# A two-block transformer kernel: high weights against high part and remainder side by side in the narrow feed-forwards, and grouped attention with two buffers of turned probabilities

## The chip, the cores and the metric

The kernel runs on one core of a Trainium2 chip. The metric is the device time of one execution in microseconds (us), lower is better. A core has TensorE (PE, matrix products, with PEld for its weight loads), VectorE (DVE), ScalarE (ACT), GpSimd (POOL) and SyncE (SP, which issues most transfers).

## The reference

All tensors are float32. There are 256 latent tokens x, 256 context tokens, and model width 1024. A first part has two layers with modulated norms and residuals, and a second part has one layer:

```
layer 0: latent attention + pooling over x and ctx, then conv feed-forward on x and on ctx
layer 1: grouped attention (8 heads of 128, 2 key heads, queries from x, keys from ctx and x), then
         xl = xl + gate * conv_ffn(modulate(xl))          # x alone: 256 tokens
conv_ffn(h): a = h @ w_up; g, u = a[:, :2816], a[:, 2816:]
         return (silu(conv3(g) + b) * u) @ w_down
second block, x alone:
         x = x + 0.5 * rmsnorm((silu(h @ wg) * (h @ wu)) @ w_down1)
         x = x + mixer(x)                                 # differential and dilated attention, gates
         x = x + 0.5 * rmsnorm((silu(h @ wg2) * (h @ wu2)) @ w_down2)
```

Each attention is softmax(q k^T * scale) v, head by head. The output is x, 256 x 1024.

## The kernel before

**Products in three parts.** Every large product is taken in fp32r with both operands split into a high part and a remainder. `three` (L342) issues three matmuls for one 128x128 tile of weights: high weights by high activations, high weights by the remainder of the activations, remainder of the weights by high activations. The three add up in one place of PSUM. The remainder by the remainder is left out.

**Weights in stripes.** The weights come from memory in stripes of 1 MB (128 x 2048), 189 in all, through a ring of three slots. SP loads `w_raw` (`load`), ACT makes `w_hi` (`split_hi`, L320), DVE makes `w_lo` (`split_lo`, L324), PE multiplies. SP waits until DVE has split the slot's last stripe, ACT waits until PE has started the stripe behind it, DVE waits for ACT, and PE waits for DVE (`begin_stripe`). Each engine runs one fixed program, written out by hand and joined to the others by semaphores, so the order on an engine is the order of the text. On ACT and DVE the split of the stripe two ahead (`ahead_hi`, `ahead_lo`) stands between the steps of the stage at hand.

**Activations.** `h_hi` and `h_lo` are 8 tiles of 128 x 512, 256 columns for the context and 256 for x. Where only x is left, the high part lies in columns 256 to 511 of `h_hi` and the remainder in the same columns of `h_lo`.

**Feed-forwards.** There are four: 0 is wide (512 columns, both token sets), 1, 2 and 3 are narrow (256 columns). 1 has the convolution; 2 and 3 are those of the second block, whose norm factor `rinv` is multiplied in behind the product. Each has 11 pairs of hidden tiles, and a pair n takes three stripes: g (gate, 2 tiles by 8 steps of k), u (up, the same) and d (down, 2 by 8 tiles). PE works on them in the order g(n+1), u(n+1), d(n); in this document d0, g1 and so on are the stripes. `up_tensor` does g and u, `down_tensor` d; the pairs 1 to 9 are a hardware loop. A narrow g goes to PSUM bank 0 and u to bank 1, two tiles of 256 columns side by side.

DVE's turn per pair (`ffn_vector`) is: `a_lo(n)` (L1595), split of d, work on g (conv L1606 behind ACT's `ffn_mid_scalar` L1547, or `ffn_scale_vector` L1619), split of the next g, work on u (`ffn_prod_vector` L1626, L1630 or L1636), split of the next u. ACT has the silu and `a_hi` (L1530), which waits until PE has finished the d before.

**Between feed-forwards 1 and 2.** Feed-forward 2 starts on activations that are not normed yet (`join_*`); the last norm of the first block is folded into a factor. Behind pair 0, DVE does two side jobs in one go: `join_x_vector` (L588, the norm applied to X), and `tables_vector` (L1882 to L1901: angles of the rotation, then lambda), which waits in its middle for ACT's sine and exponentials (`tables_scalar`, with two loads of function tables).

**Grouped attention.** `gqa_in_*` makes q, k, v from 6 stripes, PE's last one (v) in two halves; norms and rotations of the vectors run on ACT and DVE. Then for each of 8 heads: scores (L1057, two banks), row maximum (DVE L1145), exponential (ACT L1108), division by the row sum (DVE L1159), turns through the identity (PE L1076), copy of the turned probabilities to `pt_gqa` (ACT L1119, `turned_scalar`), product with v (PE L1098, `gqa_out_tensor`), split of the output (ACT L1131, DVE L1136). `pt_gqa` is one buffer. On PE head h is turns(h), scores(h+2), out(h); on ACT exp(h+1), turned(h), out_hi(h). Then `out_tensor` multiplies by four stripes of `w_out` (GO to GO+3), and `gqa_out_vector` adds to X.

## Time and profile before

| | |
|---|---|
| median of 3 runs | 1711.71 us (1711.35 to 1713.31) |
| the profiled execution: time | 1712.31 us |
| the profiled execution: span | 1709.8 us |
| PE busy | 1623.4 us, 95% of the span, 10470 matmuls |
| PE weight loads | 1408.8 us, 82% |
| DVE busy | 1040.1 us, 61% |
| ACT busy | 697.7 us, 41% |
| moved by DMA | 257.65 MB, mean 151 GB/s |

Matmuls overlap in the profile: one of 256 columns shows 283 ns from start to end while the next one starts long before. The pace is therefore read from start to start. The span of the profiled execution is 2.5 us below its time; the sums of the prediction are made against the 1712.31 us.

### The profile page before, as it was taken

How to read it: one execution, taken by the hardware profiler on the slowest of the kernel's cores; microseconds unless marked ns; L12 is line 12 of the kernel's file. 1: busy time of each engine (PE TensorE's matmuls, PEld its weight loads, DVE VectorE, ACT ScalarE, POOL GpSimd, SP SyncE). 2: the span in 40 equal slices, each digit the busy share in tenths (PEclk: the TensorE clock that was granted, in tenths of full speed). 3: DMA queues.
4: the chain of work that ended last, by engine and by line, in shares of the span. 5: the costliest groups of instructions: out<-in, count | busy, mean ns of one | idle time of the engine just before them, and what ended most of it. 6: DMA issues, size and time to landing. Idle time of an engine off the chain costs nothing.

```text
span 1709.8 us, 25411 instructions
## 1 busy us (share of the span) xinstructions
PE 1623.4 (95%) x10470; PEld 1408.8 (82%) x10470; DVE 1040.1 (61%) x1310; ACT 697.7 (41%) x879; POOL 52.2 (3%) x102
## 2 busy tenths in 40 slices
PE   6999999999999989999999989998998989889997
PEld 4655658888778868689999989997998878889997
DVE  3446436788788666546656575555664665555554
ACT  3426324233222335445444644334334654353432
POOL 1150000000000000000000000000000000000000
PEclk8999999999999999999999999998999999999999
DMA  9730452345655313034555555553545223435551
GB/s 393 272 114 1 169 207 99 131 152 167 215 197 209 107 54 124 25 99 140 180 179 189 167 172 185 183 177 98 168 151 170 75 76 122 148 123 173 192 176 49
DMA packets 168682, 257.65 MB, mean 151 GB/s; under 512 B 4160, under 2 KB 148032, under 8 KB 161824
## 3 DMA queue, kind: packets, MB, share of 16 engines
q1 hardware_dynamic: 161232, 205.21, 36.5%
q0 software_dynamic: 7232, 51.12, 8.0%
q8 instruction: 55, 0.90, 0.2%
q10 hardware_dynamic: 144, 0.26, 0.1%
q14 instruction: 19, 0.16, 0.0%
HBM read 255.53 MB, written 1.05 MB: 150 GB/s over the span
## 4 chain that ended last, share of the span: by engine, by line
PE 84%; DVE 5%; issue 5%; ACT 4%; DMA 2%; POOL 0%; SPq 0%; DVEq 0%; ACTq 0%
PE psum L342 72%; PE psum L451 2%; DMA U<-in_mod_pieces 1%; PE psum L1098 1%; ACT w_hi L320 1%; PE psum L615 1%; DVE w_lo L324 1%; DMA U<-in_w_mod 1%; PE psum L1931 1%; PE psum L2203 1%; PE psum L2182 1%; DVE scr L484 1%; PE psum L2015 0%; DVE U L484 0%; PE psum L1076 0%
## 5 line engine op out<-in xcount | busy, mean ns | idle before, releaser
L342 PE MATMUL psum<-h_hi,w_hi 128*128 128x256 f32 (+1 forms) x2176 | 690.7, 317 | 31.2 <-DVE h_lo L497 13.2
L342 PE MATMUL psum<-h_lo,w_hi 128*128 128x256 f32 (+1 forms) x2176 | 676.5, 311 | 0.0
L342 PE MATMUL psum<-h_hi,w_lo 128*128 128x256 f32 (+1 forms) x2176 | 676.4, 311 | 0.0
L324 DVE TENSOR_TENSOR w_lo<-w_raw,w_hi 128x2048 fp32r<-128x2048 f32 x189 | 433.0, 2291 | 234.6 <-ACT w_hi L320 233.1
L342 PEld LDWEIGHTS psum<-h_hi,w_hi 128*128 128x128 f32 x2176 | 420.3, 193 | 78.0 <-issue 47.1
L320 ACT ACTIVATE w_hi<-w_raw 128x2048 fp32r<-128x2048 f32 x189 | 360.6, 1909 | 290.1 <-PE psum L342 288.6
L342 PEld LDWEIGHTS psum<-h_lo,w_hi 128*128 128x128 f32 x2176 | 420.7, 193 | 23.7 <-issue 4.3
L342 PEld LDWEIGHTS psum<-h_hi,w_lo 128*128 128x128 f32 x2176 | 420.4, 193 | 20.9
L342 PE MATMUL psum<-a_hi,w_hi 128*128 128x256 f32 (+1 forms) x720 | 224.7, 312 | 6.7 <-DVE w_lo L324 4.3
L342 PE MATMUL psum<-a_lo,w_hi 128*128 128x256 f32 (+1 forms) x720 | 223.3, 310 | 0.0
L342 PE MATMUL psum<-a_hi,w_lo 128*128 128x256 f32 (+1 forms) x720 | 223.1, 310 | 0.0
L342 PEld LDWEIGHTS psum<-a_hi,w_hi 128*128 128x128 f32 x720 | 137.6, 191 | 17.2 <-DVE w_lo L324 4.5
L342 PEld LDWEIGHTS psum<-a_hi,w_lo 128*128 128x128 f32 x720 | 137.6, 191 | 7.1
L342 PEld LDWEIGHTS psum<-a_lo,w_hi 128*128 128x128 f32 x720 | 137.7, 191 | 6.5
L1530 ACT ACTIVATE a_hi<-U 128x512 fp32r<-128x512 f32 x55 | 33.6, 628 | 203.8 <-PE psum L342 186.8
L1644 DVE SCALAR_TENSOR_TENSOR X<-psum,mod,X 128x256 f32<-128x256 f32 x176 | 75.0, 479 | 26.7 <-PE psum L342 26.7
L1606 DVE SCALAR_TENSOR_TENSOR U<-psum,par,U 128x510 f32<-128x510 f32 (+1 forms) x88 | 52.1, 613 | 46.8 <-ACT U L1547 44.6
L1547 ACT ACTIVATE U<-psum,par 128x512 f32<-128x512 f32 (+1 forms) x44 | 28.3, 670 | 112.8 <-PE psum L342 112.8
L1595 DVE TENSOR_TENSOR a_lo<-U,a_hi 128x512 fp32r<-128x512 f32 x55 | 37.1, 689 | 57.6 <-ACT a_hi L1530 57.5
L658 DVE SCALAR_TENSOR_TENSOR U<-U,silu_all 128x2048 f32<-128x2048 f32 x28 | 65.2, 2347 | 0.8
L342 PE MATMUL psum<-w_hi,h_hi 128*128 128x256 f32 x144 | 41.9, 291 | 0.0
L451 PE MATMUL psum<-scr,const 128*128 128x256 f32 (+1 forms) x128 | 37.9, 450 | 4.2 <-ACT scr L426 4.2
(268 smaller groups left out, 1354.3 us busy)
## 6 DMA issues: line engine op xcount, KB each, us to landing
w_raw<-in_ffn_w_up SPq DMA_DIRECT2D x44, 1024.0 KB, 5.1
w_raw<-in_w_gu SPq DMA_DIRECT2D x44, 1024.0 KB, 5.1
U<-in_w_mod POOLq DMA_DIRECT2D x40, 1024.0 KB, 6.0
w_raw<-in_w_in SPq DMA_DIRECT2D x29, 1024.0 KB, 5.3
w_raw<-in_ffn_w_down SPq DMA_DIRECT2D x22, 1024.0 KB, 5.0
w_raw<-in_w_down SPq DMA_DIRECT2D x22, 1024.0 KB, 5.0
U<-in_mod_pieces POOLq DMA_DIRECT2D x8, 1024.0 KB, 17.8
w_raw<-in_gqa_w_in SPq DMA_DIRECT2D x6, 1024.0 KB, 5.0
```

The lines of the kernel that those rows point to most:

```text
L320: nc.scalar.activation(w_hi[:, i % RING, :], w_raw[:, i % RING, :], ACT.Copy).then_inc(hi_made, 1)
L324: nc.vector.tensor_tensor(w_lo[:, i % RING, :], w_raw[:, i % RING, :], w_hi[:, i % RING, :].bitcast(F32), ALU.subtract).then_inc(lo_made, 1)
L342: return [nc.tensor.matmul(dst, x, y, start=start and q == 0, stop=stop and q == 2, skip_group_check=True) for q, (x, y) in enumerate(pairs)]
L451: made = nc.tensor.matmul(psum[:, norm_bank(n), 0:tokens], ones, sq[:, b * T:b * T + tokens], start=c == 0 and b == 0, stop=c == chunks(n) ...
L484: made = nc.vector.scalar_tensor_tensor(out=dst, in0=x, scalar=g, in1=r, op0=ALU.mult, op1=ALU.mult)
L615: made = nc.tensor.matmul(psum[32 * j:32 * j + 32, 7, :], silu_all[:, 2 * k:2 * k + 32], w[:, TT * j:TT * (j + 1)], start=k == 0, stop=k = ...
L658: made = nc.vector.scalar_tensor_tensor(out=acc, in0=w, scalar=silu_c[:, k, s:s + 1], in1=acc, op0=ALU.mult, op1=ALU.add)
L1530: nc.scalar.activation(a_hi[:, 1 if last else t, :], f_act[:, t, :], ACT.Copy).then_inc(f_ahi, 1)
L1547: made = nc.scalar.activation(dst, src, ACT.Identity, bias=par[:, 1 + layer, bass.ds(66 + tile, 1)], scale=par[:, 1 + layer, bass.ds(NFF + ...
L1595: nc.vector.tensor_tensor(a_lo[:, at, :], f_act[:, t, :], a_hi[:, at, :].bitcast(F32), ALU.subtract).then_inc(f_alo, 1)
L1606: made = nc.vector.scalar_tensor_tensor(out=dst[:, :, dst_at:dst_at + T - 1], in0=src[:, :, src_at:src_at + T - 1], scalar=par[:, 1 + laye ...
L1644: made = nc.vector.scalar_tensor_tensor(out=x, in0=psum[:, 4 + m % 3, block_cols(s)], scalar=mod[:, 0, 40 + m, s:s + 1], in1=x, op0=ALU.mu ...
```

## The change

1. **Narrow g and u.** In the norms that feed the narrow feed-forwards (3, 4 and 8) the remainder is no longer written to `h_lo`: `h_hi[:, m, 0:256]` holds the high part and `h_hi[:, m, 256:512]` the remainder (`h_place`). A new `beside` issues two matmuls for a tile of weights: high weights by all 512 columns into a whole bank, remainder of the weights by the 256 high columns into the first half of that bank. So g has banks 0 and 1, u banks 2 and 3, and each bank holds two sums that are still to be added. `narrow_sum_vector` adds them on DVE (a tensor_reduce over two blocks, 1024 elements read from PSUM, 512 written) and its semaphores `f_gsum`, `f_usum` free the banks. What reads g or u behind it reads SBUF in place of PSUM. The down products and feed-forward 0 are as before.
2. **Side jobs of feed-forward 2.** The one block behind pair 0 is cut in four: `join_x_vector` behind pair 0, the angles behind pair 1, the sums for lambda behind pair 2, the rest behind pair 3; `tables_scalar` on ACT stands behind pair 2. The hardware loop on ACT and DVE starts at pair 4 there.
3. **Grouped attention.** `pt_gqa` becomes two buffers. The scores of heads 0 and 1 move on PE between the halves of the last stripe of `gqa_in`, behind a wait for all rotations (`gi_fix` 24), and their exponentials on ACT behind the two copies of v. In the loop PE does turns(h), scores(h+2), out(h-1), ACT turned(h), exp(h+2), out_hi(h-1), DVE max(h+2), norm(h+2), out_lo(h-1). The first stripe of `w_out` is taken apart (`gqa_merge_tensor`): tiles 0 to 4 before the turns of head 7, tile 5 behind out(6), 6 and 7 behind out(7); `out_tensor` starts at the second stripe.

```
+        def h_place(n, m, s):
+
+            if n in (3, 4, 8):
+                return h_hi[:, m, 0:T], h_hi[:, m, T:TT]
+            return h_hi[:, m, block_cols(s)], h_lo[:, m, block_cols(s)]
...
+        def beside(bank, weight, k, done=None, first=False):
+
+            wh, wl = weight
+            made = nc.tensor.matmul(psum[:, bank, :], wh, h_hi[:, k, :], start=k == 0, stop=False,
+                                    skip_group_check=True)
+            if first and k == 0:
+                made.then_inc(stripe_started, 1)
+            made = nc.tensor.matmul(psum[:, bank, 0:T], wl, h_hi[:, k, 0:T], start=False, stop=k == KD - 1,
+                                    skip_group_check=True)
+            if done is not None and k == KD - 1:
+                made.then_inc(done, 1)
...
             for t in range(4):
                 made = nc.tensor.matmul(psum[:, 4 + h % 2, 0:T], v_gqa[:, t, P * (h // 4):P * (h // 4 + 1)],
-                                        pt_g[:, t, :], start=t == 0, stop=t == 3)
+                                        pt_g[h % 2][:, t, :], start=t == 0, stop=t == 3)
...
-            need(act, at_o, 2 * (h // 2) if cfg is MLA else 8 * cfg["base"] + h)
+            need(act, at_o, 2 * (h // 2) if cfg is MLA else 8 * cfg["base"] + h - 1)
...
+        def narrow_tensor(pe, f, what, i, j, done, between):
+
+            slot = i % RING
+            need(pe, f_usum if what == "u" else f_gsum, sums_before(f) + j)
+            bank = 2 if what == "u" else 0
...
+            if what == "g" and isinstance(j, int) and j == 0:
+                for k in range(KD):
+                    h_ready(pe, FFNS[f]["norm"])(k)
+                    for t in range(2):
+                        beside(bank + t, weight(k, t), k, done if t else None, t == 0)
+                return
+            for t in range(2):
+                for k in range(KD):
+                    beside(bank + t, weight(k, t), k, done if t else None, t == 0)
+                if t == 0:
+                    between()
+
+        def narrow_sum_vector(dve, f, what, j):
+
+            bank, made = (0, f_gsum) if what == "g" else (2, f_usum)
+            dve.wait_ge(f_g if what == "g" else f_u, unit_base(f) + j + 1)
+            at = 0 if what == "g" and FFNS[f]["layer"] is None else 1
+            if what == "u":
+                dve.wait_ge(f_conv, unit_base(f) + j + 1)
+            elif at:
+                need(dve, f_prod, unit_base(f) + j)
+            nc.vector.tensor_reduce(f_act[:, at, :].rearrange("p (s t) -> p s t", s=2),
+                                    psum[:, bank:bank + 2, :].rearrange("p s (x t) -> p s t x", x=2), AX.X,
+                                    ALU.add).then_inc(made, 1)
+            dve.wait_ge(made, sums_before(f) + j + 1)
...
         def ffn_scale_vector(dve, f, j):
 
-            base = unit_base(f) + j
-            dve.wait_ge(f_g, base + 1)
-            need(dve, f_alo, base)
-            nc.vector.tensor_tensor(f_act[:, 0, :].rearrange("p (s t) -> p s t", s=2), bank2(0), double(rinv[:, 0:T]),
-                                    ALU.mult).then_inc(f_conv, 1)
+            need(dve, f_alo, unit_base(f) + j)
+            narrow_sum_vector(dve, f, "g", j)
+            g = f_act[:, 0, :].rearrange("p (s t) -> p s t", s=2)
+            nc.vector.tensor_tensor(g, g, double(rinv[:, 0:T]), ALU.mult).then_inc(f_conv, 1)
...
-            pair(0)
-            if f == 2:
-                join_x_vector(dve)
-                tables_vector(dve)
+            first = 4 if f == 2 else 1
+            parts = [lambda: join_x_vector(dve), lambda: angles_vector(dve), lambda: lambda_sums_vector(dve),
+                     lambda: lambda_vector(dve)]
+            for n in range(first):
+                pair(n)
+                if f == 2:
+                    parts[n]()
...
+                        if t == 0:
+                            pe.wait_ge(gi_fix, 24)
+                            scores_tensor(pe, GQA, 0, gqa_scores)
+                            scores_tensor(pe, GQA, 1, gqa_scores)
...
                         nc.scalar.activation(v_gqa[:, 2 * (u - 6):2 * (u - 6) + 2, :], bank2(u % 4),
                                              ACT.Copy).then_inc(gi_evac, 1)
+                        exp_scalar(act, GQA, u - 6)
...
         def gqa_tensor(pe):
-            pe.wait_ge(gi_fix, 24)
             pe.wait_ge(gi_evac, 8)
-
-            scores_tensor(pe, GQA, 0, gqa_scores)
-            scores_tensor(pe, GQA, 1, gqa_scores)
             for h in range(8):
+                if h == 7:
+                    begin_stripe(pe, GO)
+                    pe.wait_ge(at_e, at_base(GQA, n_rows) + n_rows(GQA) * 7)
+                    gqa_merge_tensor(pe, range(5))
                 turns_tensor(pe, GQA, h)
                 if h + 2 < 8:
                     scores_tensor(pe, GQA, h + 2, gqa_scores)
-                gqa_out_tensor(pe, h)
+                if h:
+                    gqa_out_tensor(pe, h - 1)
+            gqa_merge_tensor(pe, (5,))
+            gqa_out_tensor(pe, 7)
+            gqa_merge_tensor(pe, (6, 7))
```

**How the order moves.** In the rows of order a name like `psum<-h_hi,w_hi` is output, then operands, and the number behind it the columns.

PE, feed-forward 1, start of the loop over pairs 1 to 9 with the stripe g, before:

```order
L1516 UNCONDITIONAL_BRANCH
L1516 ISA
L99 REGISTER_ALU
L342 MATMUL psum<-h_hi,w_hi 128x256
L342 MATMUL psum<-h_lo,w_hi 128x256
L342 MATMUL psum<-h_hi,w_lo 128x256
L342 MATMUL psum<-h_hi,w_hi 128x256
L342 MATMUL psum<-h_lo,w_hi 128x256
```

The same place now:

```order
L1569 UNCONDITIONAL_BRANCH
L1569 ISA
L99 REGISTER_ALU
L369 MATMUL psum<-h_hi,w_hi 128x512
L373 MATMUL psum<-h_hi,w_lo 128x256
L369 MATMUL psum<-h_hi,w_hi 128x512
L373 MATMUL psum<-h_hi,w_lo 128x256
```

Three instructions of 256 columns for a tile of weights have become one of 512 and one of 256.

PE, grouped attention, the scores (L1057, now L1077), turns (L1076, now L1096) and products with v (L1098, now L1118), before:

```order
L1057 MATMUL psum<-U 128x512 x4
L1076 MATMUL psum<-const,scr 128x128 x8
L1057 MATMUL psum<-U 128x512 x2
L1098 MATMUL psum<-U 128x256 x4
L1076 MATMUL psum<-const,scr 128x128 x8
L1057 MATMUL psum<-U 128x512 x2
L1098 MATMUL psum<-U 128x256 x4
```

And now; the first row here stands behind the second half of the v stripe, and the scores of heads 0 and 1 no longer stand at its head but 48 matmuls earlier, between the halves:

```order
L1096 MATMUL psum<-const,scr 128x128 x8
L1077 MATMUL psum<-U 128x512 x2
L1096 MATMUL psum<-const,scr 128x128 x8
L1077 MATMUL psum<-U 128x512 x2
L1118 MATMUL psum<-U 128x256 x4
L1096 MATMUL psum<-const,scr 128x128 x8
L1077 MATMUL psum<-U 128x512 x2
L1118 MATMUL psum<-U 128x256 x4
```

The product with v has moved from behind its own head's turns to behind those of the next head.

DVE, feed-forward 2, from pair 0's work behind g1 to the side jobs (L324 is the split of a stripe, L1619 and L1626 the scaling of g and u, L1630 their product), before:

```order
L324 TENSOR_TENSOR w_lo<-w_raw,w_hi 128x2048
L1626 TENSOR_TENSOR U<-psum,rinv 128x512
L1630 TENSOR_TENSOR U<-U 128x512
L324 TENSOR_TENSOR w_lo<-w_raw,w_hi 128x2048
L588 SCALAR_TENSOR_TENSOR X<-X,par,rinv 128x256 x8
L1882 CAST scr<-U 128x256
L1883 TENSOR_SCALAR scr<-scr,const 128x256
```

The same place now (L331, L1674, L1681, L1684), with the sums L1491 and the split of d1 between `join_x_vector` (L608) and what follows:

```order
L331 TENSOR_TENSOR w_lo<-w_raw,w_hi 128x2048
L1491 TENSOR_REDUCE U<-psum 128x512
L1681 TENSOR_TENSOR U<-U,rinv 128x512
L1684 TENSOR_TENSOR U<-U 128x512
L331 TENSOR_TENSOR w_lo<-w_raw,w_hi 128x2048
L608 SCALAR_TENSOR_TENSOR X<-X,par,rinv 128x256 x8
L1650 TENSOR_TENSOR a_lo<-U,a_hi 128x512
L331 TENSOR_TENSOR w_lo<-w_raw,w_hi 128x2048
L1491 TENSOR_REDUCE U<-psum 128x512
```

Two reductions have come in, and `a_lo` and the split of a stripe now stand right behind `join_x_vector`, where the tables stood.

## Rows read from the trace of the kernel before

**Rows 1.** The page, part 4: the chain that ended last, by line
```profile
PE psum L342 72%; PE psum L451 2%; DMA U<-in_mod_pieces 1%; PE psum L1098 1%; ACT w_hi L320 1%; PE psum L615 1%; DVE w_lo L324 1%; DMA U<-in_w_mod 1%; PE psum L1931 1%; PE psum L2203 1%; PE psum L2182 1%; DVE scr L484 1%; PE psum L2015 0%; DVE U L484 0%; PE psum L1076 0%
```

**Rows 2.** View by windows, 800 to 900 us: busy us (x instructions) by engine, PEclk, DMA share, GB/s
```profile
800.00:900.00 100.00, 100.00 (x836) 100.00 (x835) 57.36 (x53) 45.02 (x42) 0.00 (x0) 1.00 0.56 186
```

**Rows 3.** Timeline of PE in a narrow feed-forward, 56 starts apart: start us, us, engine, line
```profile
859.75 0.28 PE L342 MATMUL psum<-h_hi,w_hi 128*128 128x256 f32 x1
...
866.47 0.28 PE L342 MATMUL psum<-h_hi,w_lo 128*128 128x256 f32 x1
```

**Rows 4.** Timeline of PE in the wide feed-forward, 14 starts apart
```profile
399.79 0.39 PE L342 MATMUL psum<-a_hi,w_hi 128*128 128x512 f32 x1
...
402.97 0.39 PE L342 MATMUL psum<-a_hi,w_lo 128*128 128x512 f32 x1
```

**Rows 5.** DVE groups by line and form: xcount | busy us, mean ns | idle before
```profile
L324 DVE TENSOR_TENSOR w_lo<-w_raw,w_hi 128x2048 fp32r<-128x2048 f32 x189 | 433.0, 2291 | 234.6 <-ACT w_hi L320 233.1
...
L1145 DVE TENSOR_REDUCE small<-psum 128x1 f32<-128x512 f32 x32 | 21.2, 687 | 7.8 <-PE psum L1057 5.5 <-PE psum L1050 2.2
...
L1619 DVE TENSOR_TENSOR U<-psum,rinv 128x512 f32<-128x512 f32 x22 | 15.2, 691 | 17.9 <-PE psum L342 16.9 <-ACT rinv L547 0.9
...
L2264 DVE TENSOR_REDUCE small<-scr 128x1 f32<-128x768 f32 x8 | 7.3, 948 | 0.1
```

**Rows 6.** Timeline, end of the first narrow feed-forward, DVE and ACT
```profile
957.82 0.69 DVE L1595 TENSOR_TENSOR a_lo<-U,a_hi 128x512 fp32r<-128x512 f32 x1
...
959.49 1.92 ACT L320 ACTIVATE w_hi<-w_raw 128x2048 fp32r<-128x2048 f32 x1 [3.39 <-PE psum L342]
```

**Rows 7.** Timeline, start of the second narrow feed-forward: DVE, PE, ACT
```profile
979.07 0.69 DVE L1619 TENSOR_TENSOR U<-psum,rinv 128x512 f32<-128x512 f32 x1 [0.93 <-ACT rinv L547]
...
987.88 2.29 DVE L324 TENSOR_TENSOR w_lo<-w_raw,w_hi 128x2048 fp32r<-128x2048 f32 x1 [1.11 <-ACT w_hi L320]
...
996.49 3.25 DVE L588 SCALAR_TENSOR_TENSOR X<-X,par,rinv 128x256 f32<-128x256 f32 x8
...
1007.53 0.15 DVE L1901 TENSOR_SCALAR small<-par 128x1 f32<-128x1 f32 x1
...
1010.89 2.29 DVE L324 TENSOR_TENSOR w_lo<-w_raw,w_hi 128x2048 fp32r<-128x2048 f32 x1 [1.10 <-ACT w_hi L320]
...
1013.23 0.58 PE L342 MATMUL psum<-a_hi,w_hi 128*128 128x256 f32 x1 [4.31 <-DVE w_lo L324]
...
1020.68 0.63 ACT L1530 ACTIVATE a_hi<-U 128x512 fp32r<-128x512 f32 x1 [4.44 <-PE psum L342]
```

**Rows 8.** View by windows, just behind PE's wait
```profile
1014.00:1016.00 2.00, 2.00 (x12) 0.50 0.61 174
```

**Rows 9.** Chain of waits through grouped attention: start us, us, what
```profile
705.50 1.72 PE psum L1057 x4
...
707.22 1.73 PE psum L1098 x8
...
708.95 0.89 PE psum L1076 x8
...
716.52 1.99 PE psum L1098 x8
...
721.30 1.99 PE psum L1098 x8
...
735.64 2.96 PE psum L1098 x8
...
742.87 23.02 PE psum L342 x192
```

**Rows 10.** Timeline: DVE's last rotation; PE at the eighth head
```profile
694.58 0.69 DVE L1823 TENSOR_TENSOR U<-U,std 128x512 f32<-128x512 f32 x1
...
735.64 1.68 PE L1098 MATMUL psum<-U 128*128 128x256 f32 x5 [1.92 <-ACT U L1119]
```

**Rows 11.** Timeline, start of the third narrow feed-forward, DVE
```profile
1516.87 0.68 DVE L1619 TENSOR_TENSOR U<-psum,rinv 128x512 f32<-128x512 f32 x1
```

146 lines of the change are left out of this document (89 added, 57 removed).

## The prediction

> **What bounds the kernel now.** First the chain that ended last: 72% of the span are split products of PE, and no other line has over 2% [rows 1]. Then the windows: in the narrow feed-forwards PE and PEld are busy for all of 100 us while DVE is busy for 57.36 and ACT for 45.02 [rows 2]. So there the pace is PE's own, and only fewer or shorter PE instructions, or the removal of PE's waits, can shorten the program. Third, the pace itself, from start to start: 56 steps of 256 columns take 866.47 - 859.75 = 6.72 us, 120.0 ns each [rows 3]; 14 steps of 512 columns take 402.97 - 399.79 = 3.18 us, 227.1 ns each [rows 4]. At 2.4 GHz the columns alone are 106.7 and 213.3 ns, so each instruction carries 13.3 or 13.8 ns on top, whatever its width. Last the two places where PE is not dense: the start of feed-forward 2, where it waits 4.31 us for the split of d1 [rows 7], and grouped attention, where a head takes 721.30 - 716.52 = 4.78 us [rows 9].
>
> **Part 1, two matmuls for three.** A tile of weights costs 3 x 120.0 = 360.0 ns before and 227.1 + 120.0 = 347.1 ns now, 12.9 ns less. There are 3 feed-forwards x 22 stripes x 16 tiles = 1056 of them: 13.6 us. In the three first stripes PE is paced by the norm that makes its activations, so their 48 tiles (0.6 us) gain nothing: **-13.0 us**. The bounds: nothing, if the time above the columns belongs to the columns or to the load of weights in a way that a longer matmul doesn't save; 26 ns a tile (-27 us) if a 256-column matmul behind a 512-column one lost its 13.3 ns too. Both rows show the surplus at equal size for both widths, so I take the middle, and a span of 10 to 14.5 us.
> The Trainium skill speaks against this size: "TensorE: Matmul & The Clock Gate", section "Back-to-back issue gap", has a warm matmul take its columns by 2.4 GHz plus about 2.5 ns, so that one matmul fewer would save 2.5 ns and the whole part 2.6 us. The trace disagrees in its premise: it has 13.3 ns where the page has 2.5 [rows 3].
>
> What it adds is the sums on DVE, 66 of them. A reduction of 512 elements from PSUM takes 687 ns and one of 768 takes 948 [rows 5], so 1.02 ns per element, and 1024 elements make **1.21 us**. Two of them raise DVE's busy time per pair from 57.36% of 17.28 = 9.9 us to 12.3, in a pair that is now 16.87 us long (32 x 347.1 + 48 x 120.0 ns). That costs nothing inside the loop: g and u have banks of their own, whose next use is two stripes (11 us) behind the end of the last one, and d(n) needs an `a_lo` that is made a pair ahead. What is queued behind the sum on DVE are the splits of the stripes; each is needed two stripes later. The DMA share of 0.56 [rows 2] leaves the loads room for the 2% faster pace.
>
> It costs something where the pipeline is short.
> - Start of 2: DVE begins the scaling of g0 at 979.07 [rows 7]; now the sum stands there, and PE's g1 waits for it until 980.3. PE is free about 979.8, an estimate: between 0 and 1.21, taken 0.5 us.
> - d0 of 2: its split at 987.88 [rows 7] comes some 1.25 us later and ends at 991.4, just when PE asks for it: 0 to 0.3, taken 0.2.
> - Start of 3: PE was already waiting for the scaling, 1516.87 to 1517.55 [rows 11]; now it waits for a sum that ends at 1518.1: 0.55.
> - Ends of 1 and 2: `a_lo` of the last pair was done at 958.51, and PE took it at about 959.4 (ACT's split, which PE's start of the last d releases, begins at 959.49) [rows 6]. The 0.9 us of slack goes against a sum of 1.21 in front: 0 to 0.5 each, taken 0.2 each. In 3 a split falls away at the end and leaves room.
>
> Together **+1.65 us** (0.5 to 3).
>
> **Part 2, the side jobs in four places.** Before, DVE did the norm (from 996.49) and the tables (to 1007.68) in one go, then `a_lo`, and only at 1010.89 the split of d1, while PE stood still for 4.31 us until 1013.23 [rows 7]. Behind it the granted clock is 0.50, which is 1.2 GHz [rows 8]: d1 takes until about 1020.6 (ACT's `a_hi` waits for its end and starts at 1020.68 [rows 7]), 7.4 us for 48 matmuls that need 5.9, so 1.5 more. Now: with four sums in front and some idle time that absorbs part of them, `join_x_vector` starts about 1000.3 and ends 1003.5; `a_lo` 0.69 and the split 2.29 end at 1006.5; PE, which had finished u2 at 1008.92 and is now some 0.6 us earlier, asks at 1008.3. Slack 1.8 us. By the same count the angles (4.6 us of DVE) leave the split of d2 a slack of 1.9, and ACT's tables, which delay `a_hi(3)` and the split of d3, leave 0.6. So no PE wait is late next: **-5.8 us** (4.5 to 6). The last slack is the one to look at.
>
> **Part 3, grouped attention.** Before, one chain ran through each head: turns, ACT's exponential, ACT's copy to the one buffer, product: 4.78 us. PE's own share is scores 1.72, product 1.73, turns 0.89 = 4.34 us [rows 9]. With a second buffer and a head between, ACT's copy has a head's time. Bounds for the new period are 4.34 and 4.78; I take 4.4, near PE's own, since maximum, exponential and division of a head now get two heads' time. At the start PE has to wait in the v stripe: the last rotation ends at 695.27 [rows 10], 2.6 us behind the end of the stripe's first half. Scores to 699.0, second half (48 x 0.12) to 704.75, copy of v, turns(0) at 705.45, a microsecond later than before; but the scores and exponentials are hidden. turns(2) then comes at 712.6, turns(6) at 730.2, product 5 ends at 732.85; 30 matmuls of `w_out` (3.6), turns(7), product 6, six more matmuls, product 7 end at 741.6; high part and remainder of the last head and its tile end at 743.4. Three stripes of 5.76 are left: 760.7. Before, the stage ended at 742.87 + 23.02 = 765.89 [rows 9]. **-5.2 us** (3 to 7). Within it is the old wait of 1.92 us at the eighth head [rows 10], behind which the product took 2.96 in place of 1.99 us [rows 9]; the stripe of `w_out` now fills it.
>
> **Sum.** -13.0 + 1.65 - 5.8 - 5.2 = -22.35 us on the profiled 1712.31: 1690.0. That execution is 0.6 us above the median of 1711.71; I forecast 1689.8.
>
> **Rivals.**
> 1. *The small parts give back* (chance 0.15). The wait of 2.6 us in the v stripe lets the clock fall as the 1.92 us at the eighth head did (+1.7), heads keep 4.78 us (4 x 0.38 = 1.5), and d3 of feed-forward 2 comes late by 3 us. For it: waits of this length have done so at two places [rows 8, 9]. Against: slack was found at each place. 1689.8 + 6.2 = 1696.
> 2. *The merged matmul saves little* (0.11): the surplus hangs on something that 512 columns behind 256 do not save. Then part 1 gives nothing: 1689.8 + 13.0 = 1702.8. Against it stands that both widths carry the same surplus [rows 3, 4]. That PE isn't the bound in g and u at all would come to the same time, and it is excluded by [rows 2]. By the rule of the Trainium skill above (same page and section) the time would be 1700.2.
> 3. *DVE becomes the pace, slower than before* (0.03). The sum reads PSUM with a stride of 256 elements, which no reduction in the trace does. If an element cost three times 1.02 ns, a sum would take 3.1 us; DVE would need 9.9 + 6.2 + some 2.5 us of waits for ACT (estimated from two such waits of 1.1 us [rows 7]) = 18.6 us a pair against PE's 16.87, 1.7 x 33 = 57 us more: 1747. It decides from 2.2 us a sum, and outweighs the gains from 2.6. Against it: 687 and 948 ns fit one line for two different shapes [rows 5].
>
> **How the numbers follow.** Forecast 0.70, rivals 0.15, 0.11, 0.03, the rest unforeseen. The forecast's bounds give 1685 to 1698, which takes in rival 1; I leave out rivals 2 and 3: 1684.5 to 1698.5. A measurement of this kernel can tell about 0.2%, 3.4 us, from no change. The forecast and rivals 1 and 2 are faster: 0.95; same 0.015, slower 0.035.
>
> **What would show it.** Right: starts 347 ns apart for a 512 and a 256 together; groups of 512 columns x1056; a sum of 1.2 us x66; PE at 100% in the loops; no wait over 1 us at d1 to d3 of feed-forward 2; heads 4.4 us apart; the stage from the v stripe's start to the last `w_out` product 5.2 us shorter. Wrong: pairs of the narrow loops not 0.41 us shorter, PE waiting for w_lo or a sum in the loop, or a granted clock of 0.5 behind the v stripe's wait.

## The result, and the profile after

The changed kernel takes **1696.67 us** in the median (1693.14 to 1698.58, 4 runs) beside 1711.53 for the kernel before on the same chip (1711.26 to 1713.31, 4 runs): ratio 0.9909, 95% interval 0.989 to 0.9928, so 14.9 us less. The forecast was 1689.8, 21.9 us below the 1711.71 that it started from. Direction and range were right; a third of the expected gain did not come.

| | before | after |
|---|---|---|
| the profiled execution: time | 1712.31 us | 1693.14 us |
| span | 1709.8 us | 1691.3 us |
| PE busy, matmuls | 1623.4 us, 10470 | 1609.9 us, 9414 |
| DVE busy | 1040.1 us | 1115.6 us |
| ACT busy | 697.7 us | 699.7 us |

That execution is the quickest of the four, 3.5 us below the median; this will matter further down.

The page of the changed kernel, part 4, the chain by line, answers to [rows 1]. The three matmuls of a tile now stand on three lines, L369 (512 columns), L373 (its 256) and L349 (what still has three), and together they keep 73% of the span:

```profile
PE psum L349 52%; PE psum L369 14%; PE psum L373 7%; PE psum L470 2%; DMA U<-in_mod_pieces 1%; PE psum L635 1%; PE psum L1077 1%; PE psum L1118 1%; DMA U<-in_w_mod 1%; ACT w_hi L327 1%; PE psum L2031 1%; PE psum L2303 1%; PE psum L2282 1%; DVE scr L503 1%; PE psum L2115 1%
```

The view by windows over the same 100 us as [rows 2]: PE is still busy throughout, with 661 matmuls for 836, and DVE has gone from 57.36 to 72.12 us. PE remained the bound of the narrow loops.

```profile
800.00:900.00 100.00, 100.00 (x661) 91.41 (x660) 72.12 (x66) 46.08 (x42) 0.00 (x0) 1.00 0.57 187
```

The groups by line show the new instructions: 1056 of each matmul, as counted, and 66 sums of 1222 ns (forecast 1.21 us).

```profile
L369 PE MATMUL psum<-h_hi,w_hi 128*128 128x512 f32 x1056 | 379.1, 402 | 12.7 <-DVE h_hi L484 7.6 <-DVE h_hi L516 3.9 <-DVE U L1491 1.2
L373 PE MATMUL psum<-h_hi,w_lo 128*128 128x256 f32 x1056 | 298.4, 283 | 0.0
L1491 DVE TENSOR_REDUCE U<-psum 128x512 f32<-128x1024 f32 x66 | 80.7, 1222 | 40.6 <-PE psum L373 39.7 <-ACT rinv L566 0.9
```

**The pace of a tile**, from PE's timeline in feed-forward 1 (start us, us, engine, line). These rows are to be read beside [rows 3, 4]. First the pair of stripes that was the only one in the loop of feed-forward 1 to run at the expected pace, then the pair behind it, which shows the pace of all others in the loop:

```profile
796.88 0.40 PE L369 MATMUL psum<-h_hi,w_hi 128*128 128x512 f32 x1
...
807.28 0.39 PE L369 MATMUL psum<-h_hi,w_hi 128*128 128x512 f32 x1
...
813.37 0.40 PE L369 MATMUL psum<-h_hi,w_hi 128*128 128x512 f32 x1
...
824.33 0.40 PE L369 MATMUL psum<-h_hi,w_hi 128*128 128x512 f32 x1
824.57 0.28 PE L373 MATMUL psum<-h_hi,w_lo 128*128 128x256 f32 x1
824.69 0.28 PE L349 MATMUL psum<-a_hi,w_hi 128*128 128x256 f32 x1
```

30 tiles in 807.28 - 796.88 = 10.40 us are 346.7 ns each, 31 tiles in 824.33 - 813.37 = 10.96 us are **353.5 ns** each. A pair of narrow stripes with its down product lasts 17.07 us (the down products begin at 1017.11 and 1034.17) where it lasted 17.28; the forecast was 16.87.

**The start of feed-forward 2**, DVE's timeline, answers to [rows 7]. The side jobs are spread, and each split (L331) before a down product is done before PE asks: PE begins its down products at 1000.05, 1017.11 and 1034.17 without a wait, 2.4, 3.0 and 2.4 us behind the end of the split. The wait of 4.31 us and the half clock behind it [rows 7, 8] are gone.

```profile
991.65 3.26 DVE L608 SCALAR_TENSOR_TENSOR X<-X,par,rinv 128x256 f32<-128x256 f32 x8
...
995.41 2.29 DVE L331 TENSOR_TENSOR w_lo<-w_raw,w_hi 128x2048 fp32r<-128x2048 f32 x1
...
1011.81 2.28 DVE L331 TENSOR_TENSOR w_lo<-w_raw,w_hi 128x2048 fp32r<-128x2048 f32 x1
...
1029.52 2.29 DVE L331 TENSOR_TENSOR w_lo<-w_raw,w_hi 128x2048 fp32r<-128x2048 f32 x1 [1.11 <-ACT w_hi L327]
```

**Grouped attention**, PE's timeline: the scores begin behind a wait for the last rotation, the first turns at 703.53, and from the third head on turns are 4.32 us apart (4.78 before [rows 9]).

```profile
693.39 3.70 PE L1077 MATMUL psum<-U 128*128 128x512 f32 x8 [2.66 <-DVE U L1892]
...
703.53 1.09 PE L1096 MATMUL psum<-const,scr 128*128 128x128 f32 x8 [0.69 <-ACT U L1865]
...
710.50 1.04 PE L1096 MATMUL psum<-const,scr 128*128 128x128 f32 x8
714.81 1.04 PE L1096 MATMUL psum<-const,scr 128*128 128x128 f32 x8
```

To say where the time went, I cut the profiled executions at PE's matmuls that begin a norm or the join. Lengths in us:

| stretch | before | after | changed kernel, second profile |
|---|---|---|---|
| grouped attention with its input and output | 140.2 | 134.6 | 136.3 |
| feed-forward 1 | 205.6 | 204.6 | 203.5 |
| feed-forward 2 | 193.1 | 185.5 | 185.5 |
| latent attention and what follows, code not changed | 324.9 | 324.5 | 324.8 |
| feed-forward 3 | 188.1 | 186.6 | 186.3 |

The second profile is that of the run e5_changed below. Feed-forward 2 gave the most, attention next, and feed-forwards 1 and 3 only 1.1 to 2.1 and 1.6 to 1.8 us.

### The profile page after: what moved, and what is told of

It reads as the page before. It is cut to its first block, busy times and chain, and to the rows that moved or that the text cites. A ratio compares the mean times of both kernels' runs of the same rounds, so it can differ in the third digit from the quotient of the medians.

```text
span 1691.3 us, 23399 instructions
## 1 busy us (share of the span) xinstructions
PE 1609.9 (95%) x9414; PEld 1348.8 (80%) x9414; DVE 1115.6 (66%) x1376; ACT 699.7 (41%) x879; POOL 52.5 (3%) x102
## 4 chain that ended last, share of the span: by engine, by line
PE 85%; issue 5%; DVE 5%; ACT 3%; DMA 2%; POOL 0%; DVEq 0%; SPq 0%; ACTq 0%
PE psum L349 52%; PE psum L369 14%; PE psum L373 7%; PE psum L470 2%; DMA U<-in_mod_pieces 1%; PE psum L635 1%; PE psum L1077 1%; PE psum L1118 1%; DMA U<-in_w_mod 1%; ACT w_hi L327 1%; PE psum L2031 1%; PE psum L2303 1%; PE psum L2282 1%; DVE scr L503 1%; PE psum L2115 1%
## 5 line engine op out<-in xcount | busy, mean ns | idle before, releaser
L331 DVE TENSOR_TENSOR w_lo<-w_raw,w_hi 128x2048 fp32r<-128x2048 f32 x189 | 432.8, 2290 | 184.8 <-ACT w_hi L327 183.1
L349 PE MATMUL psum<-h_hi,w_hi 128*128 128x256 f32 (+1 forms) x1120 | 389.0, 347 | 20.0 <-DVE h_lo L516 9.5
L369 PE MATMUL psum<-h_hi,w_hi 128*128 128x512 f32 x1056 | 379.1, 402 | 12.7 <-DVE h_hi L484 7.6
L349 PE MATMUL psum<-h_lo,w_hi 128*128 128x256 f32 (+1 forms) x1120 | 375.5, 335 | 0.0
L349 PE MATMUL psum<-h_hi,w_lo 128*128 128x256 f32 (+1 forms) x1120 | 375.3, 335 | 0.0
L373 PE MATMUL psum<-h_hi,w_lo 128*128 128x256 f32 x1056 | 298.4, 283 | 0.0
L349 PEld LDWEIGHTS psum<-h_hi,w_hi 128*128 128x128 f32 x1120 | 216.5, 193 | 64.5 <-issue 33.5
L369 PEld LDWEIGHTS psum<-h_hi,w_hi 128*128 128x128 f32 x1056 | 200.5, 190 | 63.1 <-issue 15.1
L349 PEld LDWEIGHTS psum<-h_lo,w_hi 128*128 128x128 f32 x1120 | 216.9, 194 | 23.3 <-issue 4.1
L349 PEld LDWEIGHTS psum<-h_hi,w_lo 128*128 128x128 f32 x1120 | 216.6, 193 | 20.7
L349 PE MATMUL psum<-a_hi,w_hi 128*128 128x256 f32 (+1 forms) x720 | 223.9, 311 | 2.7 <-DVE a_lo L1650 2.7
L349 PE MATMUL psum<-a_lo,w_hi 128*128 128x256 f32 (+1 forms) x720 | 222.5, 309 | 0.0
L349 PE MATMUL psum<-a_hi,w_lo 128*128 128x256 f32 (+1 forms) x720 | 222.4, 309 | 0.0
L373 PEld LDWEIGHTS psum<-h_hi,w_lo 128*128 128x128 f32 x1056 | 201.6, 191 | 0.3 <-issue 0.2
L349 PEld LDWEIGHTS psum<-a_hi,w_hi 128*128 128x128 f32 x720 | 137.1, 190 | 14.8 <-issue 3.5
L349 PEld LDWEIGHTS psum<-a_hi,w_lo 128*128 128x128 f32 x720 | 137.2, 191 | 7.0
L349 PEld LDWEIGHTS psum<-a_lo,w_hi 128*128 128x128 f32 x720 | 137.2, 191 | 6.5
L1491 DVE TENSOR_REDUCE U<-psum 128x512 f32<-128x1024 f32 x66 | 80.7, 1222 | 40.6 <-PE psum L373 39.7
```

The costliest lines, as they stand in the source:

```text
L331: nc.vector.tensor_tensor(w_lo[:, i % RING, :], w_raw[:, i % RING, :], w_hi[:, i % RING, :].bitcast(F32), ALU.subtract).then_inc(lo_made, 1)
L349: return [nc.tensor.matmul(dst, x, y, start=start and q == 0, stop=stop and q == 2, skip_group_check=True) for q, (x, y) in enumerate(pairs)]
L369: made = nc.tensor.matmul(psum[:, bank, :], wh, h_hi[:, k, :], start=k == 0, stop=False, skip_group_check=True)
L373: made = nc.tensor.matmul(psum[:, bank, 0:T], wl, h_hi[:, k, 0:T], start=False, stop=k == KD - 1, skip_group_check=True)
L1491: nc.vector.tensor_reduce(f_act[:, at, :].rearrange("p (s t) -> p s t", s=2), psum[:, bank:bank + 2, :].rearrange("p s (x t) -> p s t x", ...
```

## The experiments

Two theories, to begin with. **A, a mis-sized term:** the parts do what was forecast, but a tile saves 6.7 ns and not 12.9, because matmuls of 512 and of 256 columns alternate. **B, the clock:** the attention's wait of 2.66 us brings half clock behind it in some executions. Against both stood rival 1 of the prediction, that attention and side jobs gave their gain back. The first four kernels ran on one chip, beside a median of 1711.99 for the kernel before (7 runs), the next four on a second (1711.17, 9 runs), the last two on a third (1710.86, 15 runs). A ratio below has an interval of 0.0009 to 0.0017 to each side, 1.5 to 2.9 us, so differences between two medians of 1 to 3 us are only indications, and the pace and the stretches in the profiles say more.

### e1_three: part 1 undone

Parts 2 and 3 stay; three matmuls a tile, no sums.

```
-                    beside(bank + t, weight(k, t), k, done if t else None, t == 0)
...
+                    product(pe, psum[:, 1 if what == "u" else 0, block_cols(t)], i, t * P, h_cols(T, TT),
+                            t == 0, done if t == 1 else None)
```

> Parts 2 and 3 alone: the narrow g and u keep three matmuls of 256 columns. Theory A (the steps of the two profiles): grouped attention gives about 5.5 us and the side jobs in four places about 6, so the time is 11.5 us below the kernel before, and the changed kernel is another 6 to 8 us below this one. Rival B (the two matmuls gain their full 13 us and something else gives back): this kernel is only 5 to 6 us below before. The stripes g and u keep 360 ns a tile.

Measured: 1699.98 (1697.28 to 1702.35), ratio 0.9931 (0.9915 to 0.9948), 12.0 below the kernel before. Parts 2 and 3 together are worth what was forecast for them (11.0) within the interval. So it is part 1 that is worth too little: some 3 to 4 us net by the medians (3.3, or 3.8 by the two ratios), where the prediction had 11.35 and the expectation above 6 to 8. The stretches of this run put the parts apart: attention 136.2 us, 4.0 less than before, and feed-forward 2, which has part 2 alone here, 187.2 us, 6.0 less. Another 3.4 us of its profile are latent attention (321.5 for 324.9), whose code is the same; by the three feed-forwards alone part 1 is worth 4.3 us net in the first profile of the changed kernel and 5.5 in the second. Rival 1 falls as the explanation of the miss.

### e2_block: part 2 undone

The side jobs in one block behind pair 0.

```
-            first = 4 if f == 2 else 1
-            for n in range(first):
-                pair(n)
-                if f == 2:
-                    parts[n]()
+            pair(0)
+            if f == 2:
+                join_x_vector(dve)
+                tables_vector(dve)
```

> Parts 1 and 3 alone: the side jobs of feed-forward 2 stay in one block behind pair 0. Theory A: PE waits there as before or longer, since four sums of 1.22 us stand on DVE before the split of d1: 4.3 to 7.5 us of wait and 1.5 us at half clock, so 6 to 9 us slower than the changed kernel. Rival B (the block's cost is hidden by DVE's idle time): within 2 us of the changed kernel.

Measured: 1702.57 (1700.55 to 1703.76), ratio 0.9938. That is 5.9 us above the changed kernel's median (5.0 by the two ratios, 7.0 by the median of e5_changed), at the lower end of what was expected or a little under it. Feed-forward 2 lasts 196.2 us for 185.5, 10.7 more; the profile has latent attention 3.4 us shorter than e5_changed (321.4 for 324.8), and whether that is what keeps the medians closer was not tried. PE's timeline shows the old wait, longer than the 4.31 us before and than the 7.5 expected, since the sums stand ahead of the block too:

```profile
1011.84 0.58 PE L349 MATMUL psum<-a_hi,w_hi 128*128 128x256 f32 x1 [8.23 <-DVE w_lo L331]
```

The 5.8 us of part 2 stand, by e1_three's stretch (6.0), and beside part 1 it is worth more. Without it part 1 pays its whole gain into this wait: the three feed-forwards last 587.6 us together here, 586.9 before.

### e3_heads: part 3 undone

Grouped attention as before, parts 1 and 2 as changed.

```
-        pt_gqa = [view(4096, 1024), view(3072, 1024)]
+        pt_gqa = view(4096, 1024)
...
-                        if t == 0:
-                            pe.wait_ge(gi_fix, 24)
-                            scores_tensor(pe, GQA, 0, gqa_scores)
-                            scores_tensor(pe, GQA, 1, gqa_scores)
...
-                if h:
-                    gqa_out_tensor(pe, h - 1)
+                gqa_out_tensor(pe, h)
```

> Parts 1 and 2 alone: grouped attention as before, with one buffer and the scores behind the whole v stripe. Theory A: 5.6 us slower than the changed kernel, heads 4.78 us apart, the clock at one half for some us at the eighth head. Rival B: the scatter of the changed kernel from run to run (1693 to 1699 us) comes from a clock that falls in the wait of 2.7 us inside the v stripe; then this kernel scatters by less than 2 us and is at most 4 us slower at the median.

Measured: 1698.53 (1697.98 to 1700.17), ratio 0.9917. The stretch of attention is back at 140.2 us, against 134.6 and 136.3 in two profiles of the changed kernel, but the median is only 1.9 above the changed kernel's (1.4 by the two ratios, 3.0 by the median of e5_changed). That is less than the 5.6 us that the first profile shows and theory A expected, but two such intervals leave room for both; the size of part 3 rests on the stretches of several profiles, see theory B below.

### e4_grouped: the widths one after the other

For each half of a stripe eight matmuls of 512 columns, then eight of 256. The same matmuls, sums and data.

```
             for t in range(2):
-                for k in range(KD):
-                    beside(bank + t, weight(k, t), k, done if t else None, t == 0)
+                for part in range(2):
+                    for k in range(KD):
+                        beside(bank + t, weight(k, t), k, done if t else None, t == 0, (part,))
```

> The changed kernel with the eight matmuls of 512 columns of a tile first and its eight of 256 columns behind them, the same sums in another order. Theory A (a change of width from one matmul to the next costs 6 ns in most stripes): a tile takes 347 ns in all stripes, 1056 x 6 ns = 6 us less than the changed kernel. Rival B (the 512-column step of 234 ns comes from where the activations lie, or from DVE's reading of PSUM beside it): a tile keeps 353 ns and the time stays within 1 us.

Measured: 1691.98 (1689.62 to 1693.03), ratio 0.9878 (0.9861 to 0.9894), some 5 us less than the changed kernel by medians and ratios; the three feed-forwards are 3.1 us shorter than in e5_changed. PE's timeline in feed-forward 1 (with x8 where a row holds eight matmuls):

```profile
799.58 2.00 PE L370 MATMUL psum<-h_hi,w_hi 128*128 128x512 f32 x8
801.42 1.11 PE L376 MATMUL psum<-h_hi,w_lo 128*128 128x256 f32 x8
802.37 2.00 PE L370 MATMUL psum<-h_hi,w_hi 128*128 128x512 f32 x8
...
810.75 0.28 PE L349 MATMUL psum<-a_hi,w_hi 128*128 128x256 f32 x1
```

Eight of 512 take 1.84 us, 230 ns each, and eight of 256 take 0.95, 119 each. Over the whole pair of stripes, 32 tiles in 810.75 - 799.58 = 11.17 us, it is **349.1 ns** a tile where the alternating order has 353.5. A theory that looks for the surplus in the data, the banks or the weights themselves has no room here; the order alone makes it. Theory A holds in that, though not all of the surplus is gone: it expected 347.

### e5_changed: the changed kernel again, as yardstick of the next three

> The changed kernel as it is, on the chip of the next three, as their yardstick. Theory on the clock: PE's wait of 2.66 us in the v stripe of the grouped attention brings half clock behind it in some executions (in three of four profiles of kernels with this wait the granted clock fell to 0.66 to 0.83 between 690 and 700 us and the stage took 1.6 to 3 us more), so the runs scatter over 3 to 5 us, around 1693 to 1698, ratio about 0.991. Rival: the scatter of 5 us came from the first chip alone; then the runs lie within 2 us here.

Measured: 1695.55 (1693.63 to 1696.64, 5 runs), ratio 0.9908 (0.9894 to 0.9922). The ratio repeats, and so does the pace of 353.2 to 353.5 ns in the pairs of the loops, but for the first one in feed-forwards 2 and 3 (347). The view by windows, first of the changed kernel's first profile, then of this one (columns as in [rows 2]):

```profile
690.00:700.00 10.00, 7.34 (x41) 5.22 (x40) 7.12 (x16) 2.05 (x5) 0.00 (x0) 1.00 0.32 107
```

```profile
690.00:700.00 10.00, 7.35 (x29) 4.37 (x28) 6.64 (x13) 0.92 (x2) 0.00 (x0) 0.83 0.32 105
```

The same wait of PE was followed by a granted clock of 1.00, which is 2.4 GHz, in the one, and by stretches at 1.2 GHz in the other; the stretch of attention is 1.7 us longer there (136.3 for 134.6). e1_three, e2_block and e4_grouped, which have the same wait, had 0.83, 0.66 and 0.83 in the same window and 136.2, 137.6 and 136.3 us, and so had e8_pairs and e9_sums below (0.83, 136.2 and 136.1 us). So the first profile was the lucky one, and a typical execution gets 3.9 us out of part 3. The scatter is 3.0 us here, smaller than the 5.4 of the result's four runs.

### e6_scores: the scores 2.86 us of work later

```
                         for q in range(2):
                             c = (2 * t + q) * P
                             product_rows(pe, psum[:, u % 4, block_cols(q)], GI + s, h_cols(c, c + P),
                                          t == q == 0, True, gi_sums if q else None)
-                        if t == 0:
-                            pe.wait_ge(gi_fix, 24)
-                            scores_tensor(pe, GQA, 0, gqa_scores)
-                            scores_tensor(pe, GQA, 1, gqa_scores)
+                            if t == 1 and q == 0:
+                                pe.wait_ge(gi_fix, 24)
+                                scores_tensor(pe, GQA, 0, gqa_scores)
+                                scores_tensor(pe, GQA, 1, gqa_scores)
```

> The changed kernel with the scores of heads 0 and 1 put 2.86 us of work later in the v stripe, behind the first of the second pair of products, with the three-matmul order elsewhere as changed. Theory: the wait of 2.66 us is gone or below 0.3, with it the half clock behind it; the first turns come at about 700.9 instead of 703.5. The stage takes about 132 us (134.6 in the profile of the changed kernel, 136 to 138 with half clock); the time is 2.7 to 4.5 below the changed kernel of this chip, about 1691 to 1693, and the runs scatter over less than 3 us. Rival: the first turns wait for the exponentials of head 0, which come from the same scores, so that the wait moves there; then the time is within 1 of the changed kernel.

Measured: 1690.6 (1687.75 to 1693.8, 4 runs), ratio 0.9882, 5.0 us below e5_changed, a little more than expected. The wait is gone from PE's list of waits, the granted clock in the window is 1.00, and the stretch of attention lasts 131.7 us, 4.6 less than in e5_changed: 2.7 for the wait and 1.9 for the clock.

```profile
690.00:700.00 10.00, 10.00 (x65) 8.09 (x64) 8.17 (x14) 2.58 (x6) 0.00 (x0) 1.00 0.33 107
```

The half of the theory that spoke of the scatter was a miss: the runs lie 6 us apart, not under 3. The clock behind this wait is not what makes the runs differ most.

### e7_both: grouped widths and later scores

The edits of e4_grouped and e6_scores together.

> Eight matmuls of 512 columns and then eight of 256 for each half of a stripe (as e4_grouped), and the scores of heads 0 and 1 later (as e6_scores). If both effects stand by themselves: 4 to 5 for the grouping and 2.7 to 4.5 for the scores below the changed kernel, so 1687 to 1690, ratio 0.985 to 0.987. Rival (the grouping's gain was the clock's luck): no more than e6_scores alone gives, within 1 us of it.

Measured: 1687.74 (1686.02 to 1689.49), ratio 0.9863 (0.9848 to 0.9878), 7.8 below e5_changed and 2.9 below e6_scores. The sum came as expected, though beside e6_scores the grouping gives less than the 4 to 5 us expected, and 2.9 us between two medians is no more than their intervals allow. That it was not luck is shown by the trace: 349 ns a tile in every pair of the loops, and feed-forwards 2 and 3 each 1.1 us shorter than in e6_scores.

### e8_pairs: two and two

The order 512, 512, 256, 256: eight changes of width in 16 matmuls, where the changed kernel has sixteen and e4_grouped two. The scores stand as in the changed kernel.

```
             for t in range(2):
-                for k in range(KD):
-                    beside(bank + t, weight(k, t), k, done if t else None, t == 0)
+                for pair in range(KD // 2):
+                    for part in range(2):
+                        for k in (2 * pair, 2 * pair + 1):
+                            beside(bank + t, weight(k, t), k, done if t else None, t == 0, (part,))
```

> The changed kernel with the matmuls in the order 512, 512, 256, 256: eight changes of width in 16 matmuls where the changed kernel has sixteen and e4_grouped two. Theory A (each change between widths costs about half a nanosecond to one nanosecond, 353.2 ns a tile with all of them and 349.0 with two): 351 ns a tile, a pair of inner loops 16.97 to 17.03 long, time 2 to 3 below the changed kernel. Rival A2 (what costs is a 512 whose neighbour on both sides is a 256, whose weights change each time against a narrower cover): 349 as grouped. Rival A3 (the time of a tile is one of two values, drawn by the loop's start and not by the order): 353 or 347 in whole loops.

Measured: 1689.76 (1687.2 to 1690.58), ratio 0.9877 (0.9862 to 0.9892), 5.8 below e5_changed. PE's timeline, a row for two matmuls:

```profile
815.24 0.63 PE L370 MATMUL psum<-h_hi,w_hi 128*128 128x512 f32 x2
...
820.11 0.62 PE L370 MATMUL psum<-h_hi,w_hi 128*128 128x512 f32 x2
820.58 0.40 PE L376 MATMUL psum<-h_hi,w_lo 128*128 128x256 f32 x2
...
825.69 0.63 PE L370 MATMUL psum<-h_hi,w_hi 128*128 128x512 f32 x2
```

30 tiles in 825.69 - 815.24 = 10.45 us: 348.3 ns each, a little less than in e4_grouped with four times its changes of width. So a change of width has no price of its own, and theory A in that form, which expected 351, falls. What costs 5.2 ns is strict alternation, each 512 between two 256; that is the order of form A2, whose reason, the weights and their cover, no run shows. Rival A3 falls for this order, since every pair of the loops has the same pace; for the alternating order it is partly true (see "Left open" below). By the stretches 4.0 of the 5.8 us come from the three feed-forwards (1.2, 1.4 and 1.4). The profiled executions lie further apart than the medians, 8.4 us; 3.6 of it are latent attention (321.2 for 324.8), whose code is the same in both (see e10_best).

### e9_sums: every sum made twice

```
+            for again in range(2):
+                nc.vector.tensor_reduce(f_act[:, at, :].rearrange("p (s t) -> p s t", s=2),
+                                        psum[:, bank:bank + 2, :].rearrange("p s (x t) -> p s t x", x=2), AX.X,
+                                        ALU.add).then_inc(made, 1)
+                dve.wait_ge(made, 2 * (sums_before(f) + j) + 1 + again)
```

> The changed kernel with each of the 66 sums of DVE (1.22 us) made twice, one behind the other. Theory (a sum is paid at the starts of ff1 and ff3, where g1 waits for it, and in the first pairs of ff2, where DVE works without a pause; elsewhere it lies beside PE's work): PE's wait for the sum goes from 1.2 in all to 3.5 to 4, the first four pairs of ff2 get 4 to 7 longer, the steady pairs stay at 17.07 each; the time is 6 to 12 above the changed kernel, 1702 to 1708. Rival 3 of the prediction (DVE sets the pace of the pairs): 66 x 1.22 = 80 more. Rival (the sums hide wholly, and the shorter gain had to do with them nowhere): within 2 of the changed kernel.

Measured: 1711.49 (1709.8 to 1714.07, 10 runs), ratio 1.0007 (0.9998 to 1.0016): 15.9 above e5_changed (16.9 by the two ratios, as the chips differ), more than the 6 to 12 expected, and the whole gain of the change is gone. It is no matter of pace: DVE is busy for 84.65 of 100 us in the loop, PE for all of them, and the down products of the steady pairs stay 17.07 us apart.

```profile
850.00:950.00 100.00, 100.00 (x654) 90.98 (x653) 84.65 (x78) 45.21 (x42) 0.00 (x0) 1.00 0.58 194
```

PE's waits, first of the changed kernel (waited for: us in all, times, longest), then of this one, show where it is paid: at the ends (`a_lo`), at g1 (the sum), and for splits (`w_lo`), most of them in the first four pairs of feed-forward 2, which lasts 193.9 us for 185.5.

```profile
PE psum L349 <- DVE a_lo L1650: 2.7, 2, 2.4
...
PE psum L369 <- DVE U L1491: 1.2, 2, 0.8
...
PE psum L349 <- DVE w_lo L331: 1.0, 1, 1.0
```

```profile
PE psum L349 <- DVE a_lo L1651: 6.4, 3, 2.8
PE psum L349 <- DVE w_lo L331: 5.9, 5, 2.9
...
PE psum L369 <- DVE U L1492: 3.8, 2, 2.1
...
PE psum L369 <- DVE w_lo L331: 1.4, 1, 1.4
```

These waits are 12.6 us longer. The changed kernel has 2.4 to 3.0 us of slack left at the down products of feed-forward 2. Two more sums take 2.44 us in each pair, and where the side jobs keep DVE without a pause the delay adds up: at d0 to d3 PE waits 0.21, 0.13, 1.58 and 2.90 us here. Rival 3 of the prediction, DVE as the pace, does not come even at 2.44 us for g and as much for u, though the prediction's count had it decide from 2.2: the steady pairs keep PE's pace.

### e10_best: pairs and later scores

The edits of e8_pairs and e6_scores together.

> The changed kernel with the matmuls in the order 512, 512, 256, 256 (as e8_pairs) and the scores of heads 0 and 1 later in the v stripe (as e6_scores). If the two stand by themselves: e8_pairs' 1689.8 less 2.7 to 4.5, so 1685 to 1687, ratio about 0.985, with the attention's stage at 132 us and 348.3 ns a tile. Rival: no better than e7_both (1687.7, ratio 0.9863), since the order's gain over the grouped one is within the scatter.

Measured: **1683.93** (1683.4 to 1684.28, 5 runs), ratio 0.9842 (0.9828 to 0.9855). It is 26.9 us below the kernel before on the same chip, and 11.6 below e5_changed by their medians. It beats both kernels and is a little under the range expected. Its five runs lie 0.9 us apart. One reason for the surplus is likely in code that nobody touched, the start of latent attention; only the profiled execution shows it, and whether the other four had it is not known. Windows of 5 us that begin 15 us behind the start of that stretch, first of the changed kernel, then of e10_best:

```profile
1163.30:1168.30 5.00, 3.37 (x16) 3.40 (x17) 4.90 (x11) 3.19 (x5) 0.00 (x0) 0.52 0.00 0
```

```profile
1159.20:1164.20 5.00, 3.58 (x30) 3.61 (x31) 4.76 (x10) 3.31 (x5) 0.00 (x0) 1.00 0.00 0
```

PE works nearly as long in both, but at half clock in the one, with 16 matmuls for 30; the stretch lasts 324.5 us and 321.2. In the twelve profiles taken it was 321.2 to 321.5 us in four (e1_three, e2_block, e8_pairs, e10_best) and 323.3 to 325.2 in the other eight, the kernel before among them. The granted clock of the same window goes with it in all twelve: 1.00 in the four, 0.76 to 0.79 in e4_grouped, e6_scores and e7_both (323.3 to 323.5 us), and 0.52 to 0.60 in the other five (324.5 to 325.2 us). A difference of 2 to 4 us of this kind, together with the one behind the attention's wait, is of the size of the scatter between executions. What decides which clock comes was not tried.

## Why the prediction was right, and where it was not

**The bound.** Right. PE is dense in the narrow loops before and after, and what moved the time were PE instructions and PE waits.

**Part 1, the matmuls: the step that failed.** The forecast took "a tile of weights costs 3 x 120.0 = 360.0 ns before and 227.1 + 120.0 = 347.1 ns now". The 227.1 ns came from a place where 512 stands next to 512 [rows 4], the 120.0 from one where 256 stands next to 256 [rows 3]. In an alternating row the sum of the two is reached in one pair of stripes in the loop of feed-forward 1 and in one of feed-forward 2 of the first profile; all other pairs of the loops take 353.5. 6.5 ns by the 1008 tiles outside the three first stripes, and a little more for the quick pairs, are **some 6.8 us in place of 13.0**. The bounds given there, 0 to 26 ns, held it; the span of 10 to 14.5 us that I drew around the middle did not. Both rows showed each width among its like, and none showed the sequence that the change makes: I should have priced that as an operation not shown. e1_three, e4_grouped and e8_pairs measure it.
A saved matmul gave 6.5 ns in the alternating order and 11.7 in pairs.
The rule of the Trainium skill that the prediction quoted ("TensorE: Matmul & The Clock Gate", "Back-to-back issue gap", about 2.5 ns above the columns) would have had it give 2.5; the section limits that rule to a single matmul by itself, and the trace has a load of weights for every one.
Rival 2, at 1702.8, lay at the far end of the same line; the truth was nearly half way, at 1696.

**The first stripes.** The forecast gave them no gain. That holds for the tiles that run at half clock, which take the same time in both forms. PE's timeline at the start of feed-forward 1 of the changed kernel, and the view by windows over it with a granted clock of 0.50:

```profile
766.48 0.63 PE L369 MATMUL psum<-h_hi,w_hi 128*128 128x512 f32 x1
...
769.68 0.63 PE L369 MATMUL psum<-h_hi,w_hi 128*128 128x512 f32 x1
```

```profile
766.40:770.00 3.60, 3.60 (x13) 3.12 (x12) 3.28 (x9) 2.92 (x5) 0.00 (x0) 0.50 0.02 5
```

Five tiles in 769.68 - 766.48 = 3.20 us are 640 ns each, which is 768 columns at 1.2 GHz and nothing on top. The kernel before has a 256 every 213 ns there (774.60 and 776.52, nine apart), 640 a tile as well:

```profile
774.60 0.41 PE L342 MATMUL psum<-h_hi,w_hi 128*128 128x256 f32 x1
...
776.52 0.41 PE L342 MATMUL psum<-h_hi,w_hi 128*128 128x256 f32 x1
```

Only 8 of the 16 tiles of that stripe ran so, and 5 in e5_changed. In feed-forwards 2 and 3 the tiles of the first stripe ran at full clock, most of them in 346 to 361 ns, so a small gain was left out there, at most 0.6 us by the prediction's own count.

**Part 1, the sums.** Right in size. A sum takes 1222 ns (1.21). The busy time of DVE in a pair is 72.12% of 17.07 = 12.3 us (12.3). PE waits 0.45 us for the sum at g1 of feed-forward 2 (0.5). At g1 of feed-forward 3 it waits 0.80 us, where the kernel before waited 0.16 for the scaling, so 0.64 more (0.55):

```profile
1517.70 0.35 PE L342 MATMUL psum<-h_hi,w_hi 128*128 128x256 f32 x1 [0.16 <-DVE U L1619]
```

At the end of feed-forward 1 `a_lo` comes 0.36 late (0.2); at the end of feed-forward 2 and at its d0 nothing is late (0.2 each). Together 1.45 of the +1.65.

**Part 2.** Right. No wait at d1 to d3; slack 2.4, 3.0 and 2.4 us where 1.8, 1.9 and 0.6 were counted. The stretch is 7.6 us shorter; with 2.3 for the pace (21 stripes of 16 tiles by 6.8 ns) and the 0.45 of the sum against it, 5.8 us are left for the side jobs, as forecast. e1_three, where they stand without part 1, gives 6.0 by the same stretch.

**Part 3.** The mechanism was right step by step: a wait of 2.66 us in the v stripe (2.6), the first turns at 703.53 (705.45, in a program that was by then 1.9 us earlier), heads at 4.32 us (4.4), the stretch 5.6 us shorter (5.2). What the sum left out is the piece of rival 1 that says "the wait of 2.6 us in the v stripe lets the clock fall": it did so in six of seven profiles of kernels with this wait, and cost 1.5 to 3.0 us. That the first profile was spared, and so agreed with the forecast's 5.2, was luck. Rival 1 as a whole (1696) has the measured time, but for another reason: of its other two pieces, heads at 4.78 us and a late d3, neither came.

**The sum, mended:** -6.8 for the tiles, +1.45 for the sums, -5.8 for the side jobs and -3.9 for attention with the clock behind its wait make -15.1. The medians differ by 14.9 in the result and by 15.6 in e5_changed. These terms are read from profiles taken afterwards, so they show that the account closes, not that it could have been made blind. Of the 7.3 us between this sum and the forecast's -22.35, 6.2 are the pace of a tile and 1.3 the clock in attention; the sums on DVE cost 0.2 less than forecast.

**Left open.** It is open why strict alternation costs 5.2 ns a tile more than pairs, and what picks its pattern. Weight loads and matmuls stand in the same order in the quick and in the slow stripes, but not at the same distances. In a quick one nearly every tile takes 346 or 347 ns (in a few stripes 343 and 350 in turn). In a slow one tiles of 349, 350 and 361 ns follow each other in threes, so that it is one long step in three that makes the 353.5; PE's timeline of the changed kernel, start to start:

```profile
816.21 0.40 PE L369 MATMUL psum<-h_hi,w_hi 128*128 128x512 f32 x1
...
816.55 0.40 PE L369 MATMUL psum<-h_hi,w_hi 128*128 128x512 f32 x1
...
816.90 0.40 PE L369 MATMUL psum<-h_hi,w_hi 128*128 128x512 f32 x1
...
817.27 0.40 PE L369 MATMUL psum<-h_hi,w_hi 128*128 128x512 f32 x1
```

A pattern, once begun, lasts until other work or a wait comes between the tiles: the four stripes in front of d0 of feed-forward 1 are quick in e6_scores and slow in the changed kernel's first profile, and in the loops only the pair between d0 and d1 is quick, in some of them. So in the alternating order the time of a tile is one of two values, and nearly all pairs of the loops get the worse one; no run tried what decides. What sets the granted clock at the start of latent attention, and with it the length of that stretch, was not tried either.

## What to carry to other kernels

Price a new sequence of instructions by a row that shows that sequence, not by adding rows that show each instruction among its like; if there is none, its bounds belong in the range in full. When matmuls of two widths have to be mixed, try them in twos of one width: the edit is small and took 5.2 ns off a tile, 4.0 us off the three feed-forwards here (e8_pairs). And a wait of PE like the one of 2.66 us here is to be priced with the half clock that may follow it: putting 2.86 us of ready work in front of it (e6_scores) was worth nearly twice its length.
